# A two-layer mixer and expert kernel on eight cores: first loads reordered, zero rows moved behind them, weight copies spread, the overflow group cut into parts, buffers divided anew

## What is computed

```python
for l in range(DEPTH):                       # 2 layers, D_MODEL 1024, 4096 tokens a sequence
    m = hybrid_mixer(x, w_in[l], ...)        # z = x @ w_in (2048 columns), four head groups,
                                             # each RMS-normalised, then @ w_o
    x = layer_norm(ALPHA * x + m, ln1_g[l], ln1_b[l])
    f = grouped_moe(x, router_w, router_b, exp_w_gate[l], exp_w_up[l], exp_w_down[l])
    x = layer_norm(ALPHA * x + f, ln2_g[l], ln2_b[l])

def grouped_moe(...):                        # 16 experts in 4 groups; a token goes to the best group
    ...                                      # and there to 2 of its 4 experts
    for e in range(N_EXPERTS):
        h = jax.nn.silu(xt @ w_gate[e]) * (xt @ w_up[e])
        y = y + dense_gates[:, e:e + 1] * (h @ w_down[e])
```

## Time and profile before

| | us |
|---|---|
| median of three timed runs | 1822.36 (1813.94 to 1871.84) |
| profiled execution, its time | 1807.4 |
| its span on the slowest core (core 4) | 1806.3 |
| spans of the eight cores | 1712.5 to 1806.3 |
| PE busy on core 4 | 1307.1 of 1806.3 |
| mean granted TensorE clock on core 4 | 0.856 |

### The profile page before, as it was taken

One profiled execution on the slowest core, in us unless ns is written; L12 is line 12 of the kernel. 1 busy time (PEld: TensorE's weight loads), 2 busy tenths in 40 slices (PEclk: granted clock), 3 DMA queues, 4 the chain that ended last, 5 costly groups with the idle time before them and its releaser, 6 DMA issues. The chain is left out here.

```text
span 1806.3 us, 26074 instructions; the slowest of 8 cores (1712.5 to 1806.3 us)
## 1 busy us (share of the span) xinstructions
PE 1307.1 (72%) x7610; PEld 699.8 (39%) x7610; DVE 1008.3 (56%) x2514; ACT 655.3 (36%) x1400; POOL 201.6 (11%) x317
## 2 busy tenths in 40 slices
PE   1547587787875598998916888887874598767696
PEld 0423243333433354544503334342543354435353
DVE  0343384736666456767633375857575465554587
ACT  3323253433433423333224343533542333332222
POOL 4000010010101001111150001010101011010011
PEclk9669798888987799999967898998887698889798
DMA  9899949699209499898885907979325599664371
GB/s 193 140 192 166 155 74 155 91 140 129 71 11 179 143 192 250 206 266 258 141 187 142 148 1 102 169 98 165 88 46 123 147 203 231 167 197 129 71 272 46
DMA packets 71757, 265.63 MB, mean 147 GB/s; under 512 B 9232, under 2 KB 18064, under 8 KB 59792
## 3 DMA queue, kind: packets, MB, share of 16 engines
q0 software_dynamic: 46512, 147.84, 50.2%
q1 hardware_dynamic: 25056, 115.53, 20.7%
HBM read 327.08 MB, written 109.18 MB: 242 GB/s over the span
## 5 line engine op out<-in xcount | busy, mean ns | idle before, releaser
L1541 PE MATMUL ps<-s_k 128*128 128x384 bf16 x2048 | 348.9, 330 | 27.0 <-PEq L871 20.9
L616 PE MATMUL ps<-s_k,s_y 128*128 128x512 bf16 x1296 | 313.9, 394 | 40.3 <-issue 14.2
L616 PE MATMUL ps<-s_k 128*128 128x512 bf16 (+2 forms) x1400 | 300.0, 372 | 27.4 <-ACT s_k L664 8.7
L1541 PEld LDWEIGHTS ps<-s_k 128*128 128x128 bf16 x2048 | 201.5, 99 | 166.7 <-issue 37.0
L658 DVE SCALAR_TENSOR_TENSOR s_x<-s_x,s_sm,s_lp 128x1024 f32<-128x1024 f32 x162 | 204.2, 1277 | 12.5 <-ACT s_sm L632 9.2
L616 PEld LDWEIGHTS ps<-s_k,s_y 128*128 128x128 bf16 x1296 | 126.6, 101 | 211.0 <-issue 90.1
L616 PEld LDWEIGHTS ps<-s_k 128*128 128x128 bf16 x1400 | 137.4, 112 | 165.0 <-issue 89.1
L619 PE MATMUL ps<-s_identb,s_b 128*128 128x128 bf16 x920 | 83.9, 247 | 159.0 <-ACT s_b L664 85.4
L632 ACT ACTIVATE s_f<-ps 128x384 f32<-128x384 f32 (+2 forms) x185 | 87.9, 490 | 194.4 <-PE ps L1541 147.8
L658 DVE SCALAR_TENSOR_TENSOR s_x<-ps,s_x 128x512 f32<-128x512 f32 x192 | 134.3, 743 | 36.7 <-PE ps L616 35.6
L619 PEld LDWEIGHTS ps<-s_identb,s_b 128*128 128x128 bf16 x920 | 74.9, 151 | 180.8 <-issue 176.3
(11 more groups left out here) (159 smaller groups left out, 1225.8 us busy)
## 6 DMA issues: line engine op xcount, KB each, us to landing
s_k<-bw SPq DMA_DIRECT2D x48, 1024.0 KB, 8.2
s_x<-xs_rows SPq DMA_DIRECT2D x48, 514.0 KB, 9.6
s_k<-exp_w_gate POOLq DMA_DIRECT2D x16, 1024.0 KB, 11.9
s_k<-exp_w_up POOLq DMA_DIRECT2D x16, 1024.0 KB, 12.9
bw<-exp_w_gate POOLq DMA_DIRECT2D x16, 1024.0 KB, 22.5
bw<-exp_w_up POOLq DMA_DIRECT2D x16, 1024.0 KB, 33.0
bw<-exp_w_down POOLq DMA_DIRECT2D x16, 1024.0 KB, 30.0
s_k<-exp_w_down POOLq DMA_DIRECT2D x16, 1024.0 KB, 14.7
```

The lines of the kernel that those rows point to most:

```text
L616: pg.add(PE, lambda e: e.matmul(out.ap, lhsT.ap, rhs.ap, start=start, stop=stop), [out], [lhsT, rhs], d)
L1541: pg.add(PE, lambda en, o=o, lt=lt, rv=rv, kc=kc: en.matmul(o.v(lambda ap: ap.rearrange("p (s t) -> p s t", t=128)).ap, lt.ap, rv.ap, star ...
```

## The change

Five things. **First loads:** of the first layer's x only tile 0 is loaded at the start; the four w_in pieces are issued ahead of the parameters; the four tiles of block 1 wait for w_in[1], the norm's parameters for w_in[3]; every later block's tiles are asked for one block ahead. **Zero rows:** they are issued after the x tiles of block 2, from a buffer of pool `xo`, and the router of block 0 is written behind them. **Copies:** one at every second step of a block (`tick` at each G and O tile and after C, P and S), each waiting for the operation written before it, and in layer 0 for the last zero row, so that the 24 of them run until the last block. **Overflow:** a group is cut into load (two parts), up and down (one each per expert) and store; each part has its own branch, its own list of engines, planned at 0.25 us, and no barrier: the engines are tied by semaphores (`Chain`). `up` stands between an expert's up and down work, `down` behind it. **Buffers:** pool `f` 11 to 15, `b` 3 to 2, `gb` 4 to 2, `r` 10 to 6, `y` 3 to 2.

```diff
-        FP = pg.sbpool("f", 11, 544)
+        FP = pg.sbpool("f", 15, 544)
-        BP = pg.sbpool("b", 3, 1024, BF16)
+        BP = pg.sbpool("b", 2, 1024, BF16)
-        GB = pg.sbpool("gb", 4, 256, BF16)
+        GB = pg.sbpool("gb", 2, 256, BF16)
-        RP = pg.sbpool("r", 10, 96)
+        RP = pg.sbpool("r", 6, 96)
-        YP = pg.sbpool("y", 3, 2048, BF16)
+        YP = pg.sbpool("y", 2, 2048, BF16)
...
-        def zero_rows(after):
-            zt = Tile(XP)
-            mset(POOL, zt(), 0.0)
+        def zero_rows(deps):
+            zt = Tile(XO)
+            mset(DVE, zt(), 0.0)
...
         def copy_ahead(l, e, k):
+            deps = pg.ops[-1:]
+            if l == 0:
+                deps = deps + zeroed[-1:]
...
+        def tick(l):
+            ticks[0] += 1
+            if ahead and ticks[0] % 2 == 0:
+                copy_ahead(l, *ahead.pop(0))
...
+        def group_overflow(l, lw, g):
+            C = Chain(osem[l * 4 + g])
+            xo, to, go = Tile(XO), Tile(TP), Tile(GO)
...
+            def part(fn, w, r, engs, E):
+                def body(wait):
+                    with nc.If_cmp(regs[g], 0, "IS_GT"):
+                        wait()
+                        fn()
+                    return done(E)
+                pg.region(body, [t() for t in w], r, engs, 0.25, E)
...
+                part(fn, [xo, xb], [XSD(), ZD()], [SP, ACT], ACT)
...
+                part(fn, [b0, b1, sg, hT] + ([go] if e4 == 0 else []), [wg(), wu(), to(), cst(), xo()], [PE, ACT, DVE], DVE)
...
+                part(fn, [b0, b1, xo], [wd(), hT(), go()], [PE, DVE], DVE)
...
-                    expert(g, e4, cur, w)
-                    overflow(l, lw, g, e4, w, tl)
+                    expert(g, e4, cur, w, lambda: o_up(e4, w))
+                    o_down(e4, w)
+                    if e4 == 3:
+                        o_store()
...
-                xs = [load_x(l, i0 + r) for r in range(nt)]
+                xs = ahead_x if b else [load_x(l, i0, [])]
+                if b == 0 and l == 0:
+                    drop(0, 4)
...
-                        lw.ln1 = load_lnp(0, 0)
+                        lw.ln1 = load_lnp(0, 0, lw.after)
...
+                if not end:
+                    t1, n1 = BLOCKS[b + 1]
+                    deps = [lw.win[1].load] if l == 0 and b == 0 else pg.ops[-1:]
+                    ahead_x = [load_x(l, t1 // 128 + r, deps) for r in range(n1 // 128)]
+                    if l == 0 and b == 1:
+                        zero_rows(pg.ops[-1:])
+                        zeroed.append(pg.ops[-1])
+                        cnt, gcn = router(0, 0, *held, cnt, gcn)
```

More of the change, by code:

```diff
@@ L811, in build, with done, __init__, wait @@
         rswd = [st.enter_context(nc.semaphore("rw%d" % k)) for k in range(L)]
-        oswd = [st.enter_context(nc.semaphore("ow%d" % k)) for k in range(4 * L)]
+        osem = [[st.enter_context(nc.semaphore("og%d_%d" % (g, k))) for k in range(5)] for g in range(4 * L)]
         regs = [nc.alloc_registers("og%d" % k) for k in range(5)]
         ENGN = [E.name for E in pg.engs]
-        def done():
+        def done(E=DVE):
             marks[0] += 1
-            return nc.vector.memset(mark[0:1, marks[0] - 1:marks[0]], 0.0)
+            o = mark[0:1, marks[0] - 1:marks[0]]
+            if E is ACT:
+                return nc.scalar.copy(out=o, in_=onesb(0, 1, 0, 1).ap)
+            return E.e.memset(o, 0.0)
+        class Chain:
+            def __init__(self, sems):
+                self.sems = sems
+                self.keys = [PE, ACT, DVE, "load", "store"]
+                self.count = [0] * 5
+                self.seen = {}
+                self.hist = {}
+            def wait(self, E, k):
+                if k >= 0 and self.seen.get((E.name, k), 0) < self.count[k]:
+                    E.e.wait_ge(self.sems[k], self.count[k])
+                    self.seen[(E.name, k)] = self.count[k]
+            def do(self, E, fn, w, r, d=None):
+                need = {}
+                for lst, wr in ((r, False), (w, True)):
+                    for t in lst:
+                        for (k, kw), v in self.hist.setdefault(id(t), {}).items():
+                            if (wr or kw or t.pool.whole) and not (E is PE and self.keys[k] is PE):
+                                need[k] = max(need.get(k, 0), v)
+                for k, v in need.items():
+                    if self.seen.get((E.name, k), 0) < v:
+                        E.e.wait_ge(self.sems[k], v)
+                        self.seen[(E.name, k)] = v
+                k = self.keys.index(d or E)
+                self.count[k] += 16 if d else 1
+                ins = fn(E.e)
+                ins.then_inc(self.sems[k], 16 if d else 1)
+                for t in r:
+                    self.hist[id(t)][(k, False)] = self.count[k]
+                for t in w:
+                    self.hist[id(t)] = {(k, True): self.count[k]}
         class Steps:
@@ L1111, in load_counts @@
+            return load, up, down, store
         def load_counts(l, lw):
@@ L1521, in prep, with expert @@
                     tiles[k] = x
-            def expert(g, e4, tiles, w):
+            def expert(g, e4, tiles, w, between):
                 pos = POSA if g % 2 == 0 else POSB
@@ L1612, in mixer_layer @@
             st_.nb = 0
-            ahead = [(e, k) for e in PRE for k in range(3)]
-            ticks = made = 0
+            ahead.extend((e, k) for e in PRE for k in range(3))
+            ticks[0] = 1
             cnt, gcn = Tile(cntp), Tile(gcntp)
@@ L1646, in mixer_layer @@
                         if b:
[L1647 to L1650 removed]
+                            tick(l)
                 if end:
@@ L1666, in mixer_layer @@
                     O_tile(lw, nb, r, ys, xs[r])
+                    if b:
+                        tick(l)
                 if end:
@@ L1670, in mixer_layer @@
                     A_tile(lw, xs[r], lg, r)
-                cnt, gcn = router(l, b, lg, xs, cnt, gcn)
+                if l == 0 and b == 0:
+                    held = lg, xs
+                else:
+                    cnt, gcn = router(l, b, lg, xs, cnt, gcn)
+            assert not ahead
             ts(DVE, valid(), cnt(), iota_p, ALU.is_gt)
```

154 lines of the change are left out of this document (79 added, 75 removed).

## The result

The changed kernel takes **1716.61 us** (median of four runs, 1715.62 to 1724.6) against 1818.93 for the kernel before on the same chip: a ratio of 0.945, 95% interval 0.941 to 0.949. The medians here are over all executions of a kernel; in some of them the cores of one die show a lower granted clock and take longer, and the ratios leave those out. The forecast was 1703.

A forecast was written before the change was run, and what follows sets the result against it. PE, busy 72% of core 4's span, was taken to wait for transfers, DVE and ACT chains and the overflow group. Terms summed to -112 from 1807.4, so 1695, plus 8 for the median: 1703 us, range 1640 to 1775.

The forecast's parts named there:

- First loads, hole behind block 0, zero rows, block 1's order: Start of layer 0: earlier w_in and w_o -28, router wait filled -13, x tiles ahead of zeros -18, block 1 order -4.
- the 60 us that I had set as a sign of being wrong: First loads: the prediction called itself wrong if w_in still landed after 60 us.
- I cost that at nothing: Layer 0: block 3's x tiles wait for block 1's scatter, more than 100 us later; counted as no cost.
- Order inside the blocks, -32: Layer 0's mixer blocks: four more `f` buffers and pairs drawn apart shorten PE's waits, -32 us; upper end +15.
- Layer 1's mixer, -6: Layer 1's mixer stage: order already good, so the buffers bring little, -6 us, bounds -20 and +15.
- Smaller pools, +15 as the upper end and a rival at 1765: Layer 0's mixer: smaller pools cost more than `f` gives, a 2 to 4 us wait at each of five blocks, +15.
- Copies, +8 (0 to 30): First mixer stage: spread copies gain nothing themselves, and moving all bytes in a shorter stage is tight, +8 us, bounds 0 and 30.
- More branches, +7: PE on cores without overflow: 72 skipped parts instead of 32, at 0.33 us each, half hidden, +7 us, bounds 0 and 25.
- The overflow group, -30: Core 4's layer 1 expert stage: parts remove barriers and load ahead of time, -30 us, bounds 15 and 37 saved.
- If the cores without overflow are not faster by some 80 us: Cores without overflow: the prediction called itself wrong if they were not faster by some 80 us.
- The rival on DMA engines: First mixer stage bound by DMA engines, first expert weights and block 3's x waiting behind copies: 1730 us, chance 0.17.
- The rival on the smaller pools: Both mixers: smaller pools eat the order's gain, +24 instead of -38: 1765 us, chance 0.13.

The follow-up runs named there:

- e6: Changed kernel with buffer counts, pace of copies and overflow put back, leaving first loads, zero rows and x tiles a block ahead: 1774.0 us, 0.987 of before.
- e8: Changed kernel with layer 0's copies held to two until block 1's scatters, layer 1's in 38 steps, w_o after the last scatter: 1641.6 us, 0.912 of before.
- e7: Changed kernel with pool `f` back from 15 buffers to 11, the four smaller pools left small: 1734.97 us, 0.966 of before.
- e2: Changed kernel with all five old buffer counts (f 11, b 3, gb 4, r 10, y 3): 1777.01 us, 0.985 of before.
- e5: Kernel before with the new buffer counts alone (f 15, b 2, gb 2, r 6, y 2): 1718.48 to 1737.31 us, 0.960 of before.
- e1: Changed kernel with the old pace of weight copies, two at each G tile: 1691.66 us, 0.939 of before.
- e3: Changed kernel with the old overflow, one region per expert with barriers: 1729.87 us, 0.957 of before.
- e11: e8 with layer 0's 22 copies after the gate spread over 24 steps instead of 29: 1643.7 and 1648.4 us, 0.913 of before.
- e9: Changed kernel with `f` back to 11 and `y` back to 3, `b`, `gb` and `r` small: 1745.0 and 1757.7 us, some 0.972 of before.
- e4: Changed kernel with the 24 copies made early, over 38 of the 47 steps: 1682.48 us, 0.933 of before.

## Why the prediction came out right, and which steps of it did not

The waits that the first terms name went as forecast, but the terms don't add, and the sum came out right by errors that cancel: that is luck. On core 4, before to after, the parts of the table are -77 + 20 - 10 + 24 - 55 + 21 - 28, and 2 more at the tail: -103. The forecast was -112, and +8 for the median.

- **First loads, hole behind block 0, zero rows, block 1's order: -63 forecast.** In the changed kernel block 1's first w_o product came 65.9 us earlier. But e6, with the loads alone, gains 25 us in all where -59 stood for these parts, so most of the gain lasts only together with the other changes. The sizes inside were off as well. The first w_o product gained 19, not 28. w_in was there for POOL at 61.35, not at 56, and so beyond the 60 us that I had set as a sign of being wrong: the 8.8 MB were right (61.35 us at 143 GB/s), the rate of 159 GB/s was not. From there to the first product it took 14.5 us instead of 23.0, so 8.6 of the 12 came; the text's own figures, 23 against 20 us, had given 3. Block 0's own chain showed for 1.7 us (the wait for `s_y`).
- **"I cost that at nothing"** is the step that failed in layer 0. It weighed whether block 3's x tiles would have to wait for block 1's scatter, and ruled it out by the 100 us between them. The last of these scatters is issued at 207.0, and ACT is free for the tile at 249.5: 43 us. The scatter lands after 56, behind seven copies that had piled up on POOL, and the tile comes 19 us behind that. That is the hole of 21 us. e8 takes the pile away and the hole goes.
- **Order inside the blocks, -32.** From block 1's O products to the end of layer 0's mixer it gave 16 (364.9 to 349.1); without the hole it would be 37. Right in kind: PE's waits for DVE before the small products fell from 32.7 to 9.4 us (`s_h`, 168 to 517 us). That it was the four `f` buffers is half right: e7, with 11 of them, is slower by 2 points, and e2, with the other counts old too, by 4.
- **Layer 1's mixer, -6: the term that was wrong by most**, it gave 55. "It has the good order already" was read from one block of six, 91.8 us. e5 shows that the counts alone give 41 on core 2, e1 that the even copies give another 12. They overlap: taking the counts back (e2) costs 27 of the 55, not 41, and the loads alone (e6) give 9. The bound of -20 was too narrow as well.
- **Smaller pools, +15 as the upper end and a rival at 1765.** Wrong in sign, as far as they were tested together (e7 against e2: 2 points gained with them small). Waits for G tiles fell from 25 to 3 us with half the `gb` buffers, though not by the count alone: e1 has the same counts and 18.4 us of them. I had priced a smaller pool only as something to wait for; it also changes the order that the planner lays down. Why that order is the better one is shown for one cast (e2), and for the rest it is only seen that the waits for `s_gb` and `s_h` go (e5).
- **Copies, +8 (0 to 30).** As a total near (e1: +10), as a mechanism not. Layer 0's opening does wait for the last transfers, as the text said of the expert weights, but it is the scatter that is behind them; and it costs the same 20 us in layer 1, which the text did not look at. Against that stand 12 us gained in each mixer.
- **The boundary, nothing forecast: +24.** POOL asked for w_o 3 us ahead of the last scatter, where before it was 21 us (908.6 and 929.9). The load order of the boundary was never looked at.
- **More branches, +7.** Not seen. PE's sequencer takes 0.21 us for the median branch of L834 and 7.69 for the longest of 74. Core 1, which skips all of them, has expert stages of 303 and 301 us with the parts, and with the old regions 308 and 312 in e3 but 301 and 300 in e6. So the parts cost it 3 us at most. The Trainium skill ("Runtime: NRT & Kernel Launch", "Instruction fetch mechanics") says that a taken branch to outside the fetched window stalls for a fetch; a low median with few long branches agrees with that.
- **The overflow group, -30.** Right: 28 from before to after, 33 between e3 and after. The last expert stage of core 4 was 71 us longer than core 1's and is 40 longer now.
- **"If the cores without overflow are not faster by some 80 us"** I called myself wrong; core 1 gained 64, and the six cores without it gained 40 to 71. On core 1 the two openings and the boundary grew by 57 us, and layer 1's mixer gave 51.
- **The rival on DMA engines** (1730) did not set the time here, where block 3 ran at a DMA share of 0.71, but it is what holds e8 and e11 back in this stage. **The rival on the smaller pools** (1765) is refuted by e7 against e2.

PE's row at L834, ns min/median/max, first and last start:

```profile
L834 PEldq COMPARE_BRANCH  x74: 73/213/7690, 564.3 to 1680.5; - x74
```

What stays open: how the counts of `b`, `y`, `gb` and `r` share their 2 points, and by which step of the planner. No run moves one of them alone but `y` (e9), and the reading of the cast in e2 rests on the order in the trace, not on a run with `b` alone.

## What to carry to other kernels

List what each queue holds ahead of a transfer that somebody waits for, and hold back the bulk transfers that nobody waits for until it has been issued: with order by need in POOL's queue (and e4's pace in layer 1) the time went from 0.945 to 0.912 of before; e4's pace alone gave 0.933. When an even pace meets a gate, ask what piles up at the gate and what is issued just after it. And the number of buffers also steers a planner: dividing five pools anew, four of them smaller, gave 4% by itself (e5), so it is worth measuring both ways.

## What the runs showed of the hardware

- An indirect scatter of POOL lands in 4 to 8 us with little ahead of it in the queue (3.9 and 4.6 for the last of e11 on cores 2 and 4, a median of 7.9 in e8 behind two copies), after 22 behind three weight copies (1 MB written each) and some expert weights, 21 to 27 behind six copies asked for 33 to 45 us before (e7), 50 to 58 behind seven and 65 to 69 behind nine (core 2; 56 and 67 on core 4). What counts is when the backlog is worked off. An estimate: from the first copy to the first scatter's landing it is 66 us for six copies in e7 (159.8 to 225.8), 79 for seven in the changed kernel (170.7 to 249.4) and 101 for nine in e4 (167.3 to 268.0), all on core 2, so some 11 us a copy. It is the place in the queue more than the load of the engines: on core 2 an x tile of SP, asked for at 176.1, 2 us behind six copies of POOL, lands after 23.6 us, three more of 249.5 to 257.2 after 21.4 to 22.0, and POOL's scatters of 199 to 203 take 50 to 58. The Trainium skill ("DMA: Bandwidth & Descriptors", "Two DMAs through the same engine are not ordered") says that within one queue of a DMA engine descriptors start in order; the traces agree, with the numbers just given.
- The row of such a scatter in POOL's timeline doesn't show this: it is 1.0 us long whether it lands after 5 or after 56.
- Over layer 1's mixer the same 1980 matmuls took 347.5 us of PE at a granted clock of 0.85 before and 335.7 at 0.89 in e8: of 50 us saved there, 12 are faster matmuls, which nobody had to write. In the openings, where PE stands, the clock is 0.50.
